# Two input projections of an encoder kernel: rounded head sums two units behind, and latent units placed among gate tiles

## The reference

```
even: qa, ka, va, cq, ckv, kr, gate = split(rms_norm(x) @ w_in_ab)      # 8 dilated-window heads + 8 latent heads
      qb = rms_norm(cq) @ w_uq      -> per head 64 plain + 32 rotary columns
      kv = rms_norm(ckv) @ w_ukv    -> k and v of the latent heads; one rotary key kr for all heads
      y  = concat(out_a, out_b) * silu(gate) @ w_out_ab
odd:  q, k, v, gate = split(rms_norm(x) @ w_in_c)                       # 16 query heads, 4 key heads of 64
      q, k = rms_norm per head, then a 2-D axial rotation
      y  = (attention * silu(gate)) @ w_out_c
```

## Time and profile before

| | before |
|---|---|
| median of 3 runs | 2071.51 us (2070.16 to 2072.22) |
| the profiled execution's own time | 2070.7 us |
| its span in the profile | 2068.9 us |
| TensorE busy | 2023.8 us, 98% of the span |
| VectorE, ScalarE, GpSimd busy | 1224.0, 1127.2, 947.8 us |
| mean granted TensorE clock | 0.995 |

### The profile page before, as it was taken

One profiled execution on the slowest core, in us unless ns is written; L12 is line 12 of the kernel. 1 busy time (PEld: TensorE's weight loads), 2 busy tenths in 40 slices (PEclk: granted clock), 3 DMA queues, 4 the chain that ended last, 5 costly groups with the idle time before them and its releaser, 6 DMA issues.

```text
span 2068.9 us, 25552 instructions
## 1 busy us (share of the span) xinstructions
PE 2023.8 (98%) x9480; PEld 1629.7 (79%) x9480; DVE 1224.0 (59%) x1935; ACT 1127.2 (54%) x1440; POOL 947.8 (46%) x487
## 2 busy tenths in 40 slices
PE   8999998999999999999999999999999999999998
PEld 6878886888888877777887667888777777777888
DVE  6432135325776667663559878624477778776454
ACT  6142234435566666665446444343577778888431
POOL 1222224435555555656102556523566766677501
PEclk9999999999999999999999999999999999999999
DMA  5133468627665753734335232263233342332534
GB/s 197 56 125 128 153 241 324 169 68 156 129 120 111 169 122 85 163 77 158 120 117 185 92 108 107 102 185 102 71 77 82 72 118 71 80 87 89 169 102 168
DMA packets 172143, 261.38 MB, mean 126 GB/s; under 512 B 78754, under 2 KB 89634, under 8 KB 172020
## 3 DMA queue, kind: packets, MB, share of 16 engines
q1 hardware_dynamic: 172020, 259.76, 44.2%
HBM read 161.78 MB, written 97.92 MB: 126 GB/s over the span
## 4 chain that ended last, share of the span: by engine, by line
PE 90%; ACT 3%; DVE 2%; DMA 2%; POOL 1%; issue 1%; SPq 0%; DVEq 0%; ACTq 0%; POOLq 0%
PE SA L1926 13%; PE OP L1972 11%; PE SM L1852 5%; PE SA L533 5%; PE OP L1979 5%; PE OP L533 5%; PE SM L2025 4%; PE SA L2025 4%; PE OP L1078 4%; PE SA L1078 4%; PE OS L533 3%; PE OS L1972 3%; PE OS L1078 2%; PE OS L2025 2%; PE SM L1848 2%; PE OS L1979 1%
## 5 line engine op out<-in xcount | busy, mean ns | idle before, releaser
L2446 POOL TENSOR_TENSOR c_PL<-c_PF,c_PH 128x1024 fp32r<-128x1024 f32 x128 | 307.8, 2408 | 137.5 <-ACT c_PH L2148 79.7
L2446 POOL TENSOR_TENSOR ab_PL<-ab_PF,ab_PH 128x1024 fp32r<-128x1024 f32 (+3 forms) x128 | 264.6, 2067 | 192.4 <-ACT ab_PH L2148 135.9
L2145 ACT ACTIVATE ab_PF<-SA 128x1024 f32<-128x1024 f32 (+3 forms) x160 | 143.7, 898 | 158.3 <-PE SA L1887 85.0
L2145 ACT ACTIVATE c_PF<-SA 128x1024 f32<-128x1024 f32 x160 | 164.0, 1025 | 85.3 <-PE SA L1926 84.3
L2233 DVE TENSOR_REDUCE c_MH<-SM 128x1 f32<-128x512 f32 x256 | 170.9, 684 | 66.5 <-PE SM L1852 66.4
L431 POOL TENSOR_TENSOR e_wl<-e_raw,e_wh 128x1024 fp32r<-128x1024 f32 (+1 forms) x31 | 73.5, 2370 | 191.3 <-ACT e_wh L600 191.3
L2148 ACT ACTIVATE c_PH<-c_PF 128x1024 fp32r<-128x1024 f32 x128 | 135.8, 1061 | 4.1
L1926 PE MATMUL SA<-c_Q,c_KA 128*128 128x512 f32 x320 | 127.8, 399 | 3.3 <-ACT c_PF L2145 3.3
L1926 PE MATMUL SA<-c_Q,c_KB 72*128 72x512 f32 x320 | 127.1, 397 | 0.0
L1852 PE MATMUL SM<-c_KA,c_Q 128*128 128x512 f32 x320 | 125.1, 392 | 0.0
L1010 POOL TENSOR_TENSOR n_wl<-n_raw,n_wh 128x1024 fp32r<-128x1024 f32 (+1 forms) x24 | 53.4, 2225 | 151.5 <-ACT n_wh L1175 151.5
(11 more groups left out here) (538 smaller groups left out, 5950.9 us busy)
## 6 DMA issues: line engine op xcount, KB each, us to landing
c_Q<-qC_hi SPq DMA_DIRECT2D x32, 384.0 KB, 4.9
e_raw<-in_w_tiles SPq DMA_DIRECT2D x20, 512.0 KB, 3.9
n_raw<-in_w_tiles SPq DMA_DIRECT2D x20, 512.0 KB, 3.8
e_XF<-in_xT SPq DMA_DIRECT2D x12, 512.0 KB, 10.6
silu_gate<-e_ta SPq DMA_DIRECT2D x24, 256.0 KB, 2.1
ab_Q<-qA_hi SPq DMA_DIRECT2D x16, 384.0 KB, 5.5
ab_G<-silu_gate SPq DMA_DIRECT2D x24, 256.0 KB, 3.8
ab_res<-in_xT SPq DMA_DIRECT2D x24, 256.0 KB, 2.9
```

Source lines behind the costliest of these rows:

```text
L2145: nc.scalar.activation(used(PF[p], h, s), used(SA, h, s), ACT.Exp).then_inc(e_done, 1)
L2446: nc.gpsimd.tensor_tensor(used(PL[p], h, s), used(PF[p], h, s), used(PH[p], h, s).bitcast(F32), ALU.subtract).then_inc(p_lo[0], 1)
```

## The change

In the first projection the 42 latent units are no longer a block. After each four qB units stands one unit of gate tile 0; after each two qrB and four kB units one unit of gate tile 1; gate tile 2 stands among the vB units, where tile 0 stood. Hence `gate0` moves by six units: 15 gate units remain behind it, not 21, and `MAX0` of that layer becomes 5. The first six gates share one pair of buffers (`gate_set` is 2), and the rotations use the other two.

In the second projection the squares are rounded: ScalarE writes the square twice, to `tsq` as float32 and to `tsh` as fp32r; GpSimd subtracts them (`low_square`, right behind `rotate`, ahead of `low_weights`); TensorE sums the two parts with a rounded selection matrix in two matmuls. Every sum is made two units behind, from n = 6 on. VectorE's step n is now `low(n-4)`, `scale(n-3)`, `turn(n-1)`, and then `evict(n)`. Sums and scaled outputs stay in PSUM (banks 4 and 5); the units use banks 0 to 3. The last three units are finished at v0, with the head sums of 32 and 33 inside the first value pass.

```diff
-    U += latent_v[0:6] + [(gates[0], G0, 0)] + latent_v[6:9] + [(gates[0], G0, 1)] + latent_v[9:12] + [(gates[0], G0, 2)]
-    U += [(gates[t], G0 + t, c) for t in range(1, KT) for c in range(NC)]
+    for i in range(3):
+        U += latent_q[4 * i:4 * i + 4] + [gate_units[i]]
+    for i in range(3):
+        U += latent_r[2 * i:2 * i + 2] + latent_k[4 * i:4 * i + 4] + [gate_units[3 + i]]
+    U += latent_v[0:6] + [gate_units[6]] + latent_v[6:9] + [gate_units[7]] + latent_v[9:12] + gate_units[8:]
...
-    gate0 = gated_units[NC]
+    gate0 = gated_units[3 * NC]
...
+    def gate_set(g):
+        return 2 if g < 2 * NC else g % 3
...
-    MAX0 = 7
+    MAX0 = 5 if NA else 7
...
+    def sums_after(n):
+        return (n - 2,) if n - 2 in qk and n < v0 else ()
...
     def bank_of(n):
+        if 4 <= n < v0:
+            return n % 4
...
+        def low_square(n):
+            i = qk.index(n)
+            pool.wait_ge(q_hi, i + 1)
+            nc.gpsimd.tensor_tensor(tsl[i % 2][:], tsq[i % 2][:], tsh[i % 2][:].bitcast(F32), ALU.subtract
+                                    ).then_inc(q_lo, 1)
...
         for n in range(EARLY, N):
+            if n in qk:
+                rotate(n)
+                low_square(n)
             for w in splits[n]:
                 if w > 4:
                     low_weights(pool, w)
-            if n in qk:
-                rotate(n)
...
-            nc.tensor.matmul(sums[i % 2], sel[:], tsq[i % 2][:], start=True, stop=True).then_inc(q_sum, 1)
+            nc.tensor.matmul(sums[i % 2], selr[:], tsh[i % 2][:], start=True, stop=False)
+            pe.wait_ge(q_lo, i + 1)
+            nc.tensor.matmul(sums[i % 2], selr[:], tsl[i % 2][:], start=False, stop=True).then_inc(q_sum, 1)
...
                 for i in range(TT):
                     if q == 0 and i % 2 == 0:
-                        pe.wait_ge(acc_read, n0 + i // 2 - 5)
+                        wait_count(pe, acc_read, last_user(bank_of(n0 + i // 2), n0) + 1)
+                    if q == 0 and i in (3, 9):
+                        head_sums(v0 - 2 + i // 9)
+                    if q == 0 and i == 8:
+                        pe.wait_ge(lo_done, SCALED)
...
             nc.scalar.activation(tsq[i % 2][:], ta[place_of(i)][:], ACT.Square).then_inc(q_sq, 1)
+            nc.scalar.activation(tsh[i % 2][:], ta[place_of(i)][:], ACT.Square).then_inc(q_hi, 1)
...
+            nc.vector.tensor_tensor(scaled(i), ta[place_of(i)][:], sums[i % 2], ALU.mult).then_inc(r_norm, 1)
...
-                finish(n - 1)
-                low(n - 2)
-                low(n - 1)
+                low(n - 4)
+                scale(n - 3)
+                turn(n - 1)
+                low(n - 3)
+                for m in (n - 2, n - 1):
+                    scale(m)
+                    low(m)
+            if n in qk:
+                if n - 4 in qk:
+                    low(n - 4)
+                if n - 3 in qk:
+                    scale(n - 3)
+                if n - 1 in qk:
+                    turn(n - 1)
```

More of the change, by code:

```diff
@@ L187, in entry @@
     W = [("x", t, 8, D) for t in range(12)] + [("values", u % 4, 2, D) for u in range(8)] + [
-        ("uq", 0, 2, D), ("rope and keys", 0, 2, D), ("latent values", 0, 1, 512)] + [
-            ("x", 12 + t, 8, D) for t in range(8)]
-    V0, L0, G0 = 12, 20, 23
+        ("uq", 0, 2, D), ("x", 12, 8, D), ("rope and keys", 0, 2, D), ("x", 13, 8, D),
+            ("latent values", 0, 1, 512)] + [("x", 12 + t, 8, D) for t in range(2, 8)]
+    V0, L0 = 12, 20
+    GATE_TILE = (21, 23, 25, 26, 27, 28, 29, 30)
     U = [(tiles[t], t, c) for c in range(NC) for t in range(2)]
@@ L240, in uses, with set_uses, rope_set @@
         return sum(stage_of(j) == stage_of(i) for j in range(i))
+    def gate_set(g):
+        return 2 if g < 2 * NC else g % 3
+    def set_uses(g):
+        return sum(gate_set(j) == gate_set(g) for j in range(g))
+    def rope_set(i):
+        return i if i < NC else (i - NC) % 2
     STAT = [(c, q) for c in range(NC) for q in range(2)]
@@ L252, in entry @@
     mm_done, acc_read = ar.sem("p_mm_done"), ar.sem("p_acc_read")
-    l_sq, l_add, l_norm, l_hi, l_lo = (ar.sem(f"p_l_{n}") for n in ("sq", "add", "norm", "hi", "lo"))
+    l_sq, l_add, l_norm = (ar.sem(f"p_l_{n}") for n in ("sq", "add", "norm"))
+    l_hi, l_lo = ar.sem("p_part_hi"), ar.sem("p_part_lo")
     hi_done, lo_done = ar.sem("p_hi"), ar.sem("p_lo")
@@ L973, in sync @@
         for n in range(N):
+            if n == v0:
+                for m in range(v0 - 4, v0 - 1):
+                    store(m)
             for w in begins[n]:
@@ L976, in sync @@
                     load(sp, w + 2)
-            if n - 2 in qk:
-                store(n - 2)
+            if n - 4 in qk and n < v0:
+                store(n - 4)
+            if n == v0:
+                store(v0 - 1)
             if kind[n] == "value":
@@ L1094, in square_sum @@
         def square_sum(i, x):
-            wait_count(pe, deviation, i - 1)
-            nc.tensor.matmul(sums[i % 2], ones[:], x, start=True, stop=True).then_inc(total, 1)
+            nc.tensor.matmul(third_sum(i), ones[:], x, start=True, stop=True).then_inc(total, 1)
         def x_square_sum(c):
@@ L1192, in root @@
         out = rstd[:, cols(ORDER[i])]
-        nc.scalar.activation(out, sums[i % 2], ACT.Ln, bias=epst[:], scale=1.0 / D).then_inc(deviation, 1)
+        nc.scalar.activation(out, third_sum(i), ACT.Ln, bias=epst[:], scale=1.0 / D).then_inc(deviation, 1)
         act.wait_ge(deviation, i + 1)
@@ L1254, in scalar @@
                 high_weights(act, 4)
+            if n == 6:
                 root(act, 2)
-            for w in splits[n]:
-                if w > 4:
+            if n >= v0:
+                for w in splits[n]:
+                    if w < V0 + 2 or n > v0:
+                        high_weights(act, w)
+            if n == EARLY:
+                act.wait_ge(tab_in, 96)
+                nc.scalar.activation(selr[:], sel[:], ACT.Copy).then_inc(sel_set, 1)
+            for m in range(n - 3, n) if n == v0 else (n - 3,):
+                if m in qk and n <= v0:
+                    head_scale(m)
+                    high(m)
+            if n == v0:
+                for w in splits[v0][1:]:
                     high_weights(act, w)
-            if n - 1 in qk:
-                head_scale(n - 1)
             if n in qk:
                 square(n)
-            if n - 1 in qk:
-                high(n - 1)
+            if n < v0:
+                for w in splits[n]:
+                    if w > 4:
+                        high_weights(act, w)
             if kind[n] == "value":
@@ L1386, in vector @@
                     add_square(dve, 2, k)
-            if n - 1 in qk and n != v0:
-                finish(n - 1)
-            if n - 2 in qk and n < v0:
-                low(n - 2)
             if n in (3, 8):
```

108 lines of the change are left out of this document (61 added, 47 removed).

## The result

The changed kernel takes 2079.89 us (median of five runs, 2077.18 to 2083.63), the kernel before, on the same chip, 2071.04 us (2070.16 to 2072.22): ratio 1.0046, 95% interval 1.0034 to 1.0057, so slower by some 9 us. The forecast was 2081.5, slower by 10. The profiled execution took 2077.18 us, the lowest of the five; its span is 2075.2.

What follows compares the result with a forecast made beforehand. TensorE, busy 2023.8 of 2068.9 us, was taken as the bound. Second projection +5.5, latents -2 and head 0 +6.5 made +10 on 2070.7, with the median 0.8 higher: 2081.5 us, range 2076 to 2087 (8 in 10: 2064 to 2088).

Steps and rivals of the forecast that it cites:

- The start: Second projection, ahead of unit 7: TensorE idles 12.7 us for unit 4's low square, plus 1.5 of half clock.
- The pace: Second projection's units: the low square holds `turn`, which holds the next eviction; 6.39 us a unit against TensorE's 5.91.
- Rival (a): Second projection: `turn` gets in ahead of `low_square`, chain 5.3 us, second projection gains 13.2; 2063 us, chance 0.18.
- The end of the second projection: Value passes: third token tile waits 4.5 us for a bank; the projection ends later, taken as +5.5.
- one more half-clock stretch: End of the second projection: 6.2 us later with this further slow-clock stretch, 4.7 without it.
- First projection, latents: Latent units: late banks and weights cancel nearly all the gain; -2 us, bounds -6 and +2.
- First projection, head 0: Maxima two gates earlier find data late: TensorE waits 4.8 us plus 1.7 of half clock, +6.5.
- (b): First projection keeps up, head 0's maxima come without a wait: -6 and 0, second +5.5; 2071 us, chance 0.17.
- (c): Both projections: pauses add up, half clock behind every weight wait, head 0 at +8, second +9; 2090 us, chance 0.15.

Runs made afterwards that it cites:

- e3: Changed kernel with one more wait: GpSimd's low square of a unit starts only when VectorE's turn of that unit is done; 2065.22 us.
- e4: Changed kernel with the turn of a unit moved behind the next unit's eviction and shuffle on VectorE; 2059.52 us.
- e7: Changed kernel with head 0's first maximum one gate later (`MAX0` 6 in place of 5); 2074.73 us.
- e1: The first projection's change alone, the second projection as in the kernel before; 2073.48 us, ratio to the kernel before 1.0009.
- e2: The second projection's change alone, the first projection and `MAX0 = 7` as in the kernel before; 2080.39 us, ratio to the kernel before 1.0048.
- e5: Changed kernel with the first head sums later (those of units 4 to 7 four units behind); 2079.35 us.
- e6: Changed kernel with both the turn behind the next eviction and the first head sums later; 2055.20 us.
- e11: Changed kernel with the turn behind the next eviction, first head sums later and head 0's first maximum one gate later; 2052.27 us.
- e8: Changed kernel with ScalarE rounding the latent value weights ahead of the last high parts of the qrB group; 2080.06 us.

## Why the prediction was right

**The start.** Forecast: the sum of unit 4 released at 1146.9, unit 7 at 1147.2, `evict(6)` at 1156.8. Measured: 1146.31, 1146.90 and 1157.38, with TensorE 0.8 us earlier than before by then and `evict(4)` 0.6 (1140.51). From that eviction to the sum's release it is 5.80 us for the forecast 5.82: the chain of an eviction, two squares, two rotations and a low square was right. The half clock behind the pause was sized too small. The prediction took about 3.4 us of it, which none of its rows gives; the matmuls stood at half pace from 1146.31 to 1152.2, and unit 7 took 7.98 us in place of 5.45, which with the sum ahead of it makes 2.8 in place of 1.5. (The terms that the prediction lists for `evict(6)`, 1.5, 0.9 and 1.4 behind 1152.7, give 1156.5; its 1156.8 has 0.3 more that no term names.)

**The pace.** Forecast: 6.30 us from eviction to eviction, 6.39 with low weights. Measured: 6.30 (1202.23 to 1208.53) and 6.38 on the mean of 14 evictions. That the low square holds the turn was argued from the earlier trace rows alone, and e3 shows it: same instructions, the order fixed by one wait, turn 691 ns in place of 1683, 14.7 us less. Rival (a), in which the turn gets in ahead of the low square, is e3's case. It was right on the eviction distance (5.3) but not on what that is worth: 13.2 us of the second projection, where e3 has 8.8. It had left out the 7.0 us at each low weight tile, and e3's low square, which waits for the turn, makes the start's pause longer (8.8 and 3.9 us for 9.0 and 3.0). The 13.5 of e4 come from another way, a turn off the chain, so that they meet the 13.2 is chance.

The prediction left open whether VectorE instructions with one operand in PSUM contend with GpSimd; the trace after shows it. The eviction at 1208.53 takes 0.68 us while GpSimd's L1055 runs from 1208.02 for 2.87; the turn at 1206.90, both operands in SBUF, takes 1.71. The Trainium skill, SBUF — State Buffer, section Who interferes with whom, has this rule (at most one SBUF input, no contention; two, contention with GpSimd's reads), and the trace agrees.

**The end of the second projection.** The third value tile started at 1330.30 (1331.1 counted from where TensorE stood before) for the forecast 1330.1, behind a wait of 4.0 for 4.5. The clock was 0.83 from 1326 to 1336, the "one more half-clock stretch" that the prediction named and left out of the 4.7: the first gate behind the values starts at 1365.69 (1366.5 by the same count), not at 1364.1. The second projection cost 7.1 in the trace, forecast 5.5. Of the terms of the sum this one was low, by the half clock at two places.

**First projection, latents.** Forecast: -2, out of late banks (5 us) and late weights at the first tile-2 gate (5 us). The size was right, -3.0 up to head 0 in the trace; the place was not. There was one long wait, 6.2 us at the first vB unit, for the latent value weights, one of 0.9 for a gate tile's, and none over 0.4 for banks. These weights' rounding is queued on ScalarE behind the high part of the last rotated unit; the prediction followed that queue for a gate tile's weights only.

**First projection, head 0.** The step that was mis-sized: +6.5 (a wait of 4.8 and 1.7 of half clock). The profile shows a wait of 2.6 us, no half clock, and 3.0 in all. But other executions of the same code waited 2.8 to 5.1, and moving the maximum a gate gave 5.1 us of the median (e7). So +6.5 is too large by 1 to 2 us for the median and by 3.5 for the profiled execution. The cause stands as written: a store queued behind head 0's loads. Together, e1's +2.2 [0, 3.7] stands against a forecast of +4.5.

**The rivals.** (b), the first projection keeping up, is half of what happened in the profiled execution; it needed both terms. (c), pauses that add up to 2090, had its half clock behind four waits (9.0 with 3.0, 6.2, 4.0 and 2.3 us) but not behind the one of 2.6. What the Trainium skill, TensorE: Matmul & The Clock Gate, section HAM oscillation, says of waits between bursts of matmuls, the trace agrees with behind 9.0, 6.2 and 4.0 us. The wait of 2.6 doesn't speak against that section, whose waits are longer; it speaks against the prediction's reading, by which every wait would have brought the lower clock and the outcome would have been (c).

That the sum came out only 1.6 us above the measured median is in part luck, because its errors cancel. In the trace the second projection was low by 1.6 and the first high by 4.5 (nothing measured for +4.5); by the medians of e2 (+9.1) and e1 (+2.2) the second was low by 3.6 and the first high by 2.3. The mechanism behind the second projection's term, the pace set by the stalled turn, is not luck: e3 and e4 show it.

## What to carry to other kernels

When work is added to a helper engine, ask what it runs beside, not only how long it takes: here 1.3 us of GpSimd per unit, well inside its idle time, cost 1 us of VectorE per unit, because the two met at the same moment in every unit, and VectorE's next eviction stood in line behind that. Before giving up such a change, look at the order: one instruction moved behind the next eviction turned a loss of 9 us into a gain of 12.

A pause at the start of a pipeline is worth removing only if the engine that waits sets the pace afterwards. The same edit gave nothing in e5, where the chain was the pace, and 4 us in e6 (3 in e11).

If a kernel's runs suddenly spread, look for a compute engine that waits for a store, and then at the queue that issues it. Here the store's issue stood behind loads whose own issue took 4.6 to 6.6 us, and that was most of what varied.

## What the runs showed of the hardware

VectorE's turn has both operands in SBUF. In 29 of the 30 units it began 0.12 to 0.14 us behind GpSimd's low square and took 1.68 to 1.72 us. Once the low square had begun 0.50 us ahead of it, and it took 1.33:

```profile
1225.94 1.29 POOL L1091 TENSOR_TENSOR n_tsl<-n_tsq,n_tsh 128x512 fp32r<-128x512 f32 x1
```

```profile
1226.44 1.33 DVE L1430 TENSOR_TENSOR n_ta<-n_ta,n_tb 128x512 f32<-128x512 f32 x1
```

In all thirty the turn ends 0.54 or 0.55 us behind the low square's end, and with GpSimd held back it took 691 ns. GpSimd's own instruction kept its 1.29 us when it was first.

A wait of 2.6 us left TensorE's clock at 1.00 at 419.5. Behind one of 2.8 at the same place in e5, and one of 3.2 in e8, the mean from 412 to 432 was 0.91. In all three TensorE had paused for no longer than 0.34 us in the 50 us before. The wait of 2.3 us at 1191.8 in the changed kernel, with waits of 1.2 and 0.7 in the 30 us before it, was followed by 0.83 from 1190 to 1200. So the length of the last wait alone doesn't order these cases.
